# First weight unit loaded in two transfers, and the last gate product taken in two column groups with the final norm and store shared between engines

## What is computed

```python
# layer 0
proj = rms_norm(x) @ even_w_in          # 1024 -> 3072: retention and chunk attention
x = x + mixer(proj) @ even_w_out
x = x + hierarchical_moe(rms_norm(x))   # 16 experts, FF 512, top group then top 2
x = x + sigmoid(rms_norm(x) @ ple_w_gate) * (p[0] @ ple_w_proj)
# layer 1: the same with sliding-window attention, then
out = rms_norm(x, final_norm)
```

## Time and profile before

| | |
|---|---|
| median of 3 runs | 812.06 us (811.49 to 812.25) |
| the profiled execution's own time | 812.19 us |
| its span in the trace | 810.2 us |
| TensorE busy | 740.4 us, 91% |
| VectorE, ScalarE, GpSimd busy | 271.8, 138.1, 30.2 us |
| DMA | 245.22 MB, mean 303 GB/s |

### The profile page before, as it was taken

How to read it: one execution, slowest core, us unless ns; L and a number is a source line. 1 busy time by engine, 2 the same in 40 slices (tenths; PEclk the granted TensorE clock), 3 DMA queues, 4 the chain that set the end, 5 groups by cost and what they waited for, 6 DMA issues and landing times.

```text
span 810.2 us, 8123 instructions
## 1 busy us (share of the span) xinstructions
PE 740.4 (91%) x3080; PEld 338.8 (42%) x3080; DVE 271.8 (34%) x652; ACT 138.1 (17%) x338; POOL 30.2 (4%) x49
## 2 busy tenths in 40 slices
PE   5999999889999999888999968869999999988995
PEld 2445465564333333333445544456333333322442
DVE  0403241354326323232213351263524524232322
ACT  1100231221111111010221242222111111110121
POOL 0500000000000000000000020000000000000000
PEclk9999999979999999999999977979999999999999
DMA  9992531929999999999996092043999999999901
GB/s 335 326 335 61 199 131 49 423 89 390 420 421 421 421 420 422 421 421 411 383 235 221 28 415 104 16 192 122 423 422 421 423 419 422 421 423 420 401 29 52
DMA packets 49272, 245.22 MB, mean 303 GB/s; under 512 B 4049, under 2 KB 6449, under 8 KB 24657
## 3 DMA queue, kind: packets, MB, share of 16 engines
q1 hardware_dynamic: 47952, 242.15, 75.7%
q0 software_dynamic: 1104, 2.45, 1.0%
q10 hardware_dynamic: 176, 0.09, 0.0%
HBM read 243.61 MB, written 1.06 MB: 302 GB/s over the span
## 4 chain that ended last, share of the span: by engine, by line
PE 69%; DMA 15%; DVE 6%; SPq 5%; issue 4%; ACT 1%; POOLq 0%; POOL 0%; DVEq 0%; ACTq 0%
PE bank L569 27%; PE bank L793 17%; DMA weights<-in_moe_w_up_dram 14%; PE bank L810 9%; SPq L393 5%; PE bank L821 3%; PE bank L770 2%; PE bank L556 1%; PE bank L940 1%; DMA weights<-in_even_w_in_dram 1%; PE bank L802 1%; PE bank L603 1%; PE bank L623 1%; PE bank L998 1%; PE bank L1007 1%
## 5 line engine op out<-in xcount | busy, mean ns | idle before, releaser
L793 PE MATMUL bank<-weights,expert_rows 128*64 128x512 f32 x1024 | 227.8, 594 | 18.4 <-DMA weights<-in_moe_w_up_dram 18.4
L569 PE MATMUL bank<-weights,normalised 128*128 128x512 f32 (+1 forms) x544 | 235.7, 589 | 8.0 <-DMA weights<-in_even_w_in_dram 4.0
L569 PEld LDWEIGHTS bank<-weights,normalised 128*128 128x128 f32 x544 | 103.1, 193 | 126.0 <-issue 122.5
L793 PEld LDWEIGHTS bank<-weights,expert_rows 128*64 128x64 f32 x1024 | 75.6, 137 | 162.1 <-issue 161.9
L810 PE MATMUL bank<-weights,hidden_turned 128*64 128x512 f32 x512 | 116.9, 598 | 2.5 <-DVE hidden_turned L1613 1.9
L1613 DVE COPY hidden_turned<-bank 128x256 f32<-128x256 f32 x32 | 13.6, 425 | 185.8 <-PE bank L802 185.8
L810 PEld LDWEIGHTS bank<-weights,hidden_turned 128*64 128x64 f32 x512 | 34.7, 136 | 67.4 <-issue 67.4
L1214 ACT ACTIVATE gate_tanh<-bank 128x256 f32<-128x256 f32 x32 | 12.3, 385 | 209.7 <-PE bank L793 209.7
L1086 ACT ACTIVATE expert_outputs<-bank 128x512 fp32r<-128x512 f32 x32 | 19.1, 597 | 127.8 <-PE bank L810 127.8
L1643 DVE TENSOR_TENSOR gather_onehots<-bank,expert_outputs 128x512 fp32r<-128x512 f32 x32 | 22.1, 690 | 51.6 <-ACT expert_outputs L1086 51.5
L1625 DVE SCALAR_TENSOR_TENSOR spread_gates<-token_slots,router_temps,token_gates 128x512 f32<-128x512 f32 x32 | 24.1, 752 | 19.8 <-ACT token_gates L1206 18.7
(11 more groups left out here) (231 smaller groups left out, 524.2 us busy)
## 6 DMA issues: line engine op xcount, KB each, us to landing
weights<-in_moe_w_gate_dram SPq DMA_DIRECT2D x64, 1024.0 KB, 21.2
weights<-in_moe_w_up_dram SPq DMA_DIRECT2D x64, 1024.0 KB, 23.3
weights<-in_moe_w_down_dram SPq DMA_DIRECT2D x64, 1024.0 KB, 24.2
weights<-in_even_w_in_dram SPq DMA_DIRECT2D x6, 2048.0 KB, 18.3
weights<-in_ple_w_gate_dram SPq DMA_DIRECT2D x4, 2048.0 KB, 30.9
weights<-in_even_w_out_dram SPq DMA_DIRECT2D x2, 2048.0 KB, 18.0
weights<-in_odd_w_qkv_dram SPq DMA_DIRECT2D x2, 2048.0 KB, 18.7
weights<-in_odd_w_out_dram SPq DMA_DIRECT2D x4, 1024.0 KB, 21.0
```

The costliest lines, as they stand in the source:

```text
L569: mm = pe.matmul(B[bank][:, 0:width], XT[:, k, tok(t)], w[:, k, :], start=(k == 0), stop=(k == KD - 1))
L793: mm = pe.matmul(bank[j * BLK:(j + 1) * BLK, :].rearrange("p (m f) -> p m f", m=2), rows[:, k, :], W[:, slots, a:a + FF // 2], start=(k == ...
```

## The change

SyncE loads unit 0 as two DMAs, steps 0 to 3 and steps 4 to 7 of the contraction, with a semaphore of its own for the second. The product waits for the first half, runs four matmuls, waits for the second half and runs the other four. Every other product goes through the same helper without the second wait.

In layer 1 the last gate product runs as two groups of 8 matmuls of 256 columns, into banks 7 and 5. Tanh and the update run per group. The square runs over 768 elements behind the first group and over 256 behind the second, each with its own sum. VectorE multiplies the first 768 elements by the norm's weights while the second group still runs. Behind the power, ScalarE scales elements 0 to 511, VectorE does the whole product for 768 to 1023 and scales 512 to 767. The tile is stored as two DMAs, elements 512 to 1023 first. In two other places a named semaphore is replaced by the common counter of VectorE's steps (`then`).

```diff
-            cols(U_IN, even_w_in[0], order[0])
+            for half in range(2):
+                sp.dma_start(unit(U_IN).rearrange("p (k n) -> p k n", k=KD)[:, 4 * half:4 * half + 4, :],
+                             even_w_in[0][:, order[0]:order[0] + 512].rearrange("(p k) n -> p k n", p=P)
+                             [:, 4 * half:4 * half + 4, :]).then_inc((landed(U_IN)[0], sem("first_unit_rest"))[half], 16)
...
-            for t in range(TT):
-                sp.wait_ge(sem("out_ready"), t + 1)
-                sp.dma_start(out[0, tok(t), :], OUTB[:, t, :]).then_inc(sem("stored"), 16)
-            sp.wait_ge(sem("stored"), 32)
+            sp.wait_ge(sem("out_ready"), 1)
+            sp.dma_start(out[0, tok(0), :], OUTB[:, 0, :]).then_inc(sem("stored"), 16)
+            sp.wait_ge(sem("out_ready"), 2)
+            sp.dma_start(out[0, tok(1), 512:D], OUTB[:, 1, 512:D]).then_inc(sem("stored"), 16)
+            sp.wait_ge(sem("out_by_act"), 1)
+            sp.dma_start(out[0, tok(1), 0:512], OUTB[:, 1, 0:512]).then_inc(sem("stored"), 16)
+            sp.wait_ge(sem("stored"), 48)
...
+            def project_part(n, t, bank, half, done, width=512, first=0):
+
+                if half == 0:
+                    s, v = landed(n)
+                    pe.wait_ge(s, v)
+                elif n == U_IN:
+                    pe.wait_ge(sem("first_unit_rest"), 16)
+                w = unit(n)[:, first:first + KD * width].rearrange("p (k n) -> p k n", k=KD)
+                for k in range(4 * half, 4 * half + 4):
+                    mm = pe.matmul(B[bank][:, 0:width], XT[:, k, tok(t)], w[:, k, :], start=(k == 0), stop=(k == KD - 1))
+                if half == 1:
+                    mm.then_inc(sem(done), 1)
+
             def project_rows(n, t, bank, done, width=512, first=0):
-
-                s, v = landed(n)
-                pe.wait_ge(s, v)
-                w = unit(n)[:, first:first + KD * width].rearrange("p (k n) -> p k n", k=KD)
-                for k in range(KD):
-                    mm = pe.matmul(B[bank][:, 0:width], XT[:, k, tok(t)], w[:, k, :], start=(k == 0), stop=(k == KD - 1))
-                mm.then_inc(sem(done), 1)
+                for half in range(2):
+                    project_part(n, t, bank, half, done, width, first)
...
-                project_rows(gate + 1, 1, 7, "pg_ready")
+                if l == 0:
+                    project_rows(gate + 1, 1, 7, "pg_ready")
+                else:
+                    s, v = landed(gate + 1)
+                    pe.wait_ge(s, v)
+                    w = unit(gate + 1).rearrange("p (k n) -> p k n", k=KD)
+                    for c, bank in enumerate((7, 5)):
+                        if c == 1:
+                            pe.wait_ge(sem("pg_tanh"), 6)
+                        for k in range(KD):
+                            mm = pe.matmul(B[bank][:, 0:256], XT[:, k, tok(1)], w[:, k, 256 * c:256 * c + 256],
+                                           start=(k == 0), stop=(k == KD - 1))
+                        mm.then_inc(sem("pg_ready"), 1)
...
-            gate_tanh(1, 1, 1)
-            squares(6, 1)
+            for c, bank in enumerate((7, 5)):
+                act.wait_ge(sem("pg_ready"), 8 + c)
+                act.activation(THG[:, 1, 512 + 256 * c:768 + 256 * c], B[bank][:, 0:256], ACT.Tanh, scale=rstd(5, 1))\
+                    .then_inc(sem("pg_tanh"), 1)
+                act.wait_ge(sem("h_updates"), h_done(5, 1) + c)
+                act.wait_ge(sem("squares_ready"), 13 + c)
+                a, b = (0, 768) if c == 0 else (768, D)
+                act.activation(JUNK[:, a:b], H[:, 1, a:b], ACT.Square, accum_out=(ST[:, 6, 1:2], LASTSQ)[c])\
+                    .then_inc(sem("squares_ready"), 1)
+            act.wait_ge(sem("rstd_ready"), 14)
+            act.wait_ge(sem("weighted"), 1)
+            act.activation(OUTB[:, 1, 0:512], OUTB[:, 1, 0:512], ACT.Copy, scale=rstd(6, 1)).then_inc(sem("out_by_act"), 1)
...
-            update(1, 1, 1)
-            mean_square(6, 1)
-            finished(1)
+            dve.wait_ge(sem("fw_landed"), 16)
+            for c in range(2):
+                a = slice(512 + 256 * c, 768 + 256 * c)
+                dve.wait_ge(sem("pg_tanh"), 8 + c)
+                then(dve.scalar_tensor_tensor(out=THG[:, 1, a], in0=THG[:, 1, a], scalar=1.0, in1=B[3][:, 256 * c:256 * c + 256],
+                                              op0=ALU.add, op1=ALU.mult))
+                dve.scalar_tensor_tensor(out=H[:, 1, a], in0=THG[:, 1, a], scalar=0.5, in1=H[:, 1, a],
+                                         op0=ALU.mult, op1=ALU.add).then_inc(sem("h_updates"), 1)
+                if c == 0:
+                    dve.wait_ge(sem("h_updates"), h_done(5, 1))
+                    dve.tensor_tensor(OUTB[:, 1, 0:768], H[:, 1, 0:768], FW[:, 0:768], ALU.mult).then_inc(sem("weighted"), 1)
+                    dve.wait_ge(sem("squares_ready"), 14)
+                    then(dve.tensor_scalar(FIRSTSQ, ST[:, 6, 1:2], 1.0 / D, EPS, ALU.mult, ALU.add))
+            dve.wait_ge(sem("squares_ready"), 15)
+            dve.tensor_scalar(ST[:, 6, 3:4], LASTSQ, 1.0 / D, FIRSTSQ, ALU.mult, ALU.add).then_inc(sem("ms_ready"), 1)
+            dve.wait_ge(sem("rstd_ready"), 14)
+            dve.wait_ge(sem("weighted"), 1)
+            dve.wait_ge(sem("h_updates"), h_done(5, 1) + 1)
+            dve.scalar_tensor_tensor(out=OUTB[:, 1, 768:D], in0=H[:, 1, 768:D], scalar=rstd(6, 1), in1=FW[:, 768:D],
+                                     op0=ALU.mult, op1=ALU.mult)
+            dve.tensor_scalar(OUTB[:, 1, 512:768], OUTB[:, 1, 512:768], rstd(6, 1), None, ALU.mult).then_inc(sem("out_ready"), 1)
```

More of the change, by code:

```diff
@@ L216, in build @@
         TH, AG, US = (sb(name, [P, 256])[:, :] for name in ("gate_tanh", "gate_silu", "hidden"))
+        LASTSQ, FIRSTSQ = RT[:, 0:1], RT[:, 1:2]
         SM = RT[:, 80:144].rearrange("p (n h) -> p n h", n=4)
@@ L1417, in gated @@
                 dve.wait_ge(sem("rg_tanh"), t + 1)
-                dve.scalar_tensor_tensor(out=GATE[:, t, :], in0=THR[:, t, :], scalar=1.0, in1=B[2 + t][:, :],
-                                         op0=ALU.add, op1=ALU.mult).then_inc(sem("gate_ready"), 1)
-                dve.wait_ge(sem("gate_ready"), t + 1)
+                then(dve.scalar_tensor_tensor(out=GATE[:, t, :], in0=THR[:, t, :], scalar=1.0, in1=B[2 + t][:, :],
+                                              op0=ALU.add, op1=ALU.mult))
                 dve.scalar_tensor_tensor(out=RET[:, t, :], in0=RET[:, t, :], scalar=rstd(0, t), in1=GATE[:, t, :],
@@ L1580, in experts @@
                 then(dve.tensor_tensor(O2, O2, SLT, ALU.mult))
-                dve.tensor_reduce(S2, O2, AX.X, ALU.add).then_inc(sem("slots_ready"), 1)
-                dve.wait_ge(sem("slots_ready"), l + 1)
+                then(dve.tensor_reduce(S2, O2, AX.X, ALU.add))
                 dve.wait_ge(sem("iota_ready"), l + 1)
```

## The result

The changed kernel took 807.88 us as the median of 4 executions (806.23 to 808.59), the kernel before 812.15 beside it (4 executions, 811.49 to 812.69). The ratio is 0.9945, 95% interval 0.9927 to 0.9963: 4.3 us faster, where 3.1 had been summed. The profiled execution took 808.59 with a span of 806.6.

A forecast was written before the change was run, and what follows sets the result against it. TensorE, busy 91% of the span, was taken as the bound, with its waits at start and end paid in full. Gains of 1.29 and 1.84 sum to 3.13 us, giving 808.9 from the median of 812.06; range 807.9 to 810.6.

The forecast's parts named there:

- the start: First product: starts at 10.02 in place of 11.31, when ScalarE's copies end; gain 1.29 us.
- The second half, the x rows and the second unit: Loads behind the first half: delayed by at most 0.65 us, all landing before they are wanted; cost nothing.
- Rival C's first form: Start: first half lands with the whole because packets mix; C as a whole: gain 1.5 to 1.9 us, chance 0.14.
- the tail: Chain after the last product: first store issued at 805.35 in place of 807.19; gain 1.84 us.
- the two bounds: Stores of half a tile: full 2.6 us each, tail gain 1.45; or 0.65 less, tail gain 2.10.
- the 256-column groups: Layer 1's last gate product: two groups take 6.86 us against 6.88, so TensorE ends at the same time.
- rival D: Last product: weight loads of the 256-column groups no longer hidden, 6.1 us more, 815.0 in all; chance 0.04.
- the range: Whole kernel: 807.9 to 810.6 us, from the tail's bounds, the clock's spread, rival B and half of C.
- a spread of half a microsecond from the clock's rises: Whole kernel: with the tail's bounds it widens the forecast to 808.1 to 809.8 us.
- The sum: Both ends of the kernel: 1.29 at the start plus 1.84 at the tail, 3.13 us; forecast chance 0.55.
- Rival B: Clock rises keep their time, so the start's gain shrinks to 0.1 to 0.65 us; 809.6 to 810.1, chance 0.27.
- the prediction's own sign: Gather products: 1.3 us earlier if the forecast holds; less than 0.7 earlier shows it wrong.

The follow-up runs named there:

- the dummies' kernels: Changed kernel, once the kernel before, with dummy matmuls in TensorE's start, router or attention pauses, singly, paired or all; ratios 0.9873 to 0.9964 against the kernel before.
- the separate parts: Kernel before with only the first unit in two transfers, ratio 0.9986; kernel before with only the new tail, ratio 0.9979.
- dummies on both sides: Kernel before with dummy matmuls in start, router and attention pauses, mean 804.57 us, against the changed kernel with dummies in all three, mean 801.41.
- all of them: Changed kernel with dummy matmuls ahead of the first product and in the router and attention pauses; ratios 0.9877 and 0.9873 against the kernel before, mean 801.41 us.
- start and router alone: Changed kernel with dummy matmuls only ahead of the first product, mean 808.71 us, or only in both layers' router pauses, mean 807.74 us.
- attention alone: Changed kernel with dummy matmuls only in three TensorE pauses of layer 1's attention; ratio 0.9924 against the kernel before, mean 805.81 us.

## Why the prediction was right and wrong

**Right: the start.** The first half was to land near 8.5 and landed at 8.2; TensorE was to start at 10.02 and started at 9.43 to 9.99 in all traces with the split. The kernels with one transfer started at 11.31, 10.96 and 10.96, and 9.88, 9.69, 9.60, 9.82 and 9.43 with two: 1.4 on average against 1.29 (without the dummies' kernels). It was still there behind the first product, whose length varied from 8.59 to 10.18 in these traces: the next products started at 22.07, 23.20 and 22.78 with one transfer, mean 22.68, and at 21.29 on average in the nine traces with two and no dummies ahead. Alone it measured 1.5 +- 0.4. The second half, the x rows and the second unit (landed at 3.42 + 15.1 = 18.5) were never waited for. Rival C's first form did not occur: the two halves landed 2.6 apart.

**Right: the tail.** From tanh to first store 3.78 was summed and 3.69 measured (803.49 - 799.80). Within it tanh was 0.47 for the 0.39 taken from a form without a scale per token, the power's follower came 0.08 sooner and the last two VectorE steps took 0.78 with the issue, for 0.87. The second store came 0.39 later, and landed 2.3 after its issue, between the two bounds (1.95 and 2.6); the first landed 2.0 after its own. Gain to the landing: (807.19 + 2.6 - 801.57) - (803.88 + 2.3 - 799.80) = 8.22 - 6.38 = 1.84, the value taken. The Trainium skill, "DMA: Bandwidth & Descriptors", section on the anatomy of one DMA, whose fixed cost plus bytes gave an estimated 2.6 for a half store, was 0.3 over, as it was over for the whole one; by it the gain would have been 1.45.

**Right: the 256-column groups** kept their loads hidden, so rival D did not occur; the cover of the first group's chain was 0.84 for a predicted 0.7.

**Wrong: the range.** The step that failed is "a spread of half a microsecond from the clock's rises". What the runs show in its place is a standard deviation of 1.1 to 1.6 us over executions, in 20 and 104 of them. The prediction had three executions of before within 0.8 us and no other source for the half microsecond. It also put the whole spread down to the clock, while the traces show a second source beside it, VectorE's steps that run into GpSimd's add, worth 2 to 4 us of the attention when they do. With four executions a median is easily 0.7 off; 807.88 was such a draw, and the three samples of the changed kernel gave 807.88, 808.67 and 808.06. Pooled, the mean of 808.19 and the median of 808.5 lie inside the range and 0.4 to 0.7 below the forecast of 808.9. That the single number fell just outside is luck; that it could is the mis-sized term.

**The sum.** 3.13 was forecast. The pooled difference of means is 811.88 - 808.19 = 3.7 +- 0.3, the separate parts give 3.5 +- 0.6, and with dummies on both sides 3.2 +- 0.9. The rows of the two touched places account for 1.4 + 1.8 = 3.2 of it. The remaining 0.5 has no row of its own and is under two standard errors.

**Rival B** was half right. Its mechanism is real: in the first trace after, the start's gain was taken back whole by a later rise, and 2.35 us came back in a product of layer 1. By the prediction's own sign (gather products starting less than 0.7 earlier) that trace spoke for B, with 168.02 against 168.06 in layer 0. But the rises do not keep their time in the span: in traces of the same kernel they were at 14.4 and 16.7, and at 15.7 and 14.4. So the start's gain can be lost in a single execution and came out whole over many. The Trainium skill, "TensorE: Matmul & The Clock Gate", part 1, says that the monitor is free-running and that the count of slow matmuls varies from run to run; the traces agree, with a first product of 8.59 and of 10.09 in one kernel. It advises not to fit to a count, which should have warned the prediction against a range of half a microsecond.

## What to carry to other kernels

A gain of a few microseconds that is read from serial rows at the two ends of a kernel can be trusted step by step. The time of a few executions could not show it here, where TensorE has pauses of 2 to 4 us behind which the clock may be at either level, and where a VectorE step and a GpSimd step start within 0.3 us of each other in either order. Look for such pauses and such near ties before giving a range, and compare stages between traces, engine by engine, not spans: equal TensorE rows do not mean that the clock is the only difference. Where a pause can't be removed, dummy matmuls in it may be worth more than the tuning at hand: here all of them brought 6.8 us over the changed kernel, and 10.5 over the one before (811.88 - 801.41), though no run here tells what dummies cost that outlast the wait. Moving GpSimd's add away from VectorE's steps is the untested next try.

## What was not expected of the hardware

A VectorE step that starts just behind a GpSimd step can take as long as that step: 128x512 took 2.76 in place of 0.69, and 128x4 took 2.32 in place of 0.16, beside GpSimd adds of 2.3 to 2.8 us that had begun 0.14 and 0.19 ahead. In traces of equal kernels it comes with an attention stage some 2 to 4 us longer. Layer 1's attention took 154.0 us without it and with its output products at 7.1, 157.1 with one of them at 9.4, up to 158.5 with the collision, and 150.4 with the clock at 2.4 GHz throughout. Dummies in single places did not add up: start and router alone changed the total by +0.5 +- 0.5 and -0.5 +- 0.5 though their own stages became about 2 us shorter, attention alone brought 2.4 and all together 6.8. And a store of 256 KB issued 0.39 us behind another of the same size still ended no earlier than one of 512 KB issued at the first one's time.
